# First mixer without GpSimd sums; second block's attention units between its projection steps

## The chip, the cores and the metric

One NeuronCore of one Trainium2 chip. The metric is the device time of one execution in microseconds, the median over runs. TensorE (PE) multiplies, VectorE (DVE), ScalarE (ACT) and GpSimd (POOL) do the rest, and their instructions are ordered among each other by semaphores alone.

## The reference

Two models, one after the other, on 256 tokens of width 1024, all in float32.

- The first has two layers with modulation: `cond @ ada_w` gives shift, scale and gate for each half layer. Layer 0 mixes by 16 attention heads of width 64 with a relative position bias and a block-causal band, layer 1 by spatial gating. Both have a squared-ReLU MLP of width 4096.
- The second has two layers. Each norms x, projects it to aq, ak, av, ag (512 each), bq (512), bk, bv (128 each) and bg (512), and does

```python
lam = exp(sum(lp[0] * lp[1])) - exp(sum(lp[2] * lp[3])) + lam_init
p = softmax(aq_h @ ak_h.T * 64 ** -0.5 + bias)   # 4 heads, two components each
oa = (p[0] - lam * p[1]) @ av_h                  # one value product of the difference
ya = rms_norm(oa, gain) * (1 - lam_init) * silu(ag)
yb = (softmax(q @ k.T * 64 ** -0.5) @ bv) * silu(bg)   # 8 query heads, 2 key heads, RoPE
x = x + rms_norm(concat(ya, yb) @ w_out, gain)
```

## The kernel before

**Precision.** A product of float32 matrices is done by `matmul3` (L1493 to L1495) as three float32r matmuls: high by high, high by low, low by high. Weights come in chunks of 128x2048 in two halves: a transfer into `raw` (4 half slots, SP queue), ScalarE's copy to `w_hi` (L552, `hi_part`), VectorE's difference to `w_lo` (L916, `lo_part`), 4 chunk slots. A projection of 512 columns takes two chunks and 4 steps of 12 matmuls (half, token tile).

**Modulation.** `adastream` holds 48 chunks of 1 MB, loaded by GpSimd's queue into the two slots of `ada_raw`. VectorE sums the 8 tiles of a chunk, each times its column of `cond`, in two accumulators (`ada_sum`, L939 to L947), and counts the chunk in `s_ada`, for which the next loads of GpSimd's queue wait.

**First mixer.** A loop over h = 0 to 18 is written out for all engines. TensorE does a projection or output step, the value product of head h-3, the scores of head h and the transposes of head h-2. VectorE adds the bias and takes the minimum of the negated scores (L1172), ScalarE exponentiates (L671) and copies transposed probabilities (L666), VectorE normalises (L1133). `head_square`, GpSimd's reciprocals (`head_rinv`), `q_heads` (L1036), a transpose, `unit_hi` (L634) and `unit_lo` (L1108) make the operands of scores. Of the modulation chunks 10 to 18, VectorE sums the even ones: 10 whole, ahead of `unit_lo(4)` and `unit_lo(5)`, and 12, 14, 16, 18 in quarters, one to a head. GpSimd sums the odd ones 11, 13, 15, 17 (`pool_sum`, L453 to L459).

**Second block**, for each of two layers. Projections of bk and bv, bq, aq, ak, av, ag, bg come first (the last two are `lproject(12)` and `lproject(14)`), then 16 units (8 differential: head and component; 8 grouped), then both output projections (`lproject(16)` and `lproject(18)`). Iteration i of the unit loop on TensorE:

```python
# i < 8: the bias through the flipped identity, then the fp32 product, in one bank
nc.tensor.matmul(dst, flip[:], t5_h[:, hh, at:at + S], start=True, stop=False)
last = nc.tensor.matmul(dst, aqT[lanes, hh, seg * P:(seg + 1) * P], akT[lanes, hh, :], ...)
# unit i-1: four transposes (L1957); unit i-2: four value products (L1978)
```

VectorE takes the maximum (L1414), copies transposed probabilities out of PSUM (L1424), and scales the outputs by the reciprocal sums, combining the two components of a head in `y_a` (L1434, L1442) and gating `y_b` (L1453). ScalarE exponentiates (L871) and squares `y_a` (L883). GpSimd makes the reciprocals and gates `y_a` (L526, L530) once, after all four heads. `keep_warm` (L1578) adds a small matmul to the late units. After it come the transposes of `y_a` and `y_b`, their high and low halves, and the output projections.

## Time and profile before

| what | value |
|---|---|
| time, median of 3 runs | 1172.77 us (1171.68 to 1174.82) |
| profiled execution, its own time | 1173.97 us |
| its span | 1172.3 us |
| mean granted clock of TensorE | 0.958 |
| TensorE, VectorE, ScalarE, GpSimd busy | 1124.2, 770.9, 527.9, 132.1 us |
| first mixer's head loop | about 87.6 to 189.7 us in the span |
| from ag's projection to the last output matmul | 890.8 to 994.4 and 1060.9 to 1164.6 us |

The span runs from the first to the last instruction; the time of an execution also has what lies around it. Matmuls are pipelined: the duration of one is longer than the distance to the next, so costs on TensorE are read from start to start. The granted clock is given as a share of 2.4 GHz.

### The profile page before, as it was taken

To read this page: it belongs to the slowest core of one execution; us is meant where nothing else is said; L and a number is where in the kernel's file an instruction comes from. 1 tells how busy PE (TensorE), PEld (TensorE's weight loads), DVE (VectorE), ACT (ScalarE), POOL (GpSimd) and SP (SyncE) were. 2 spreads that over 40 slices of the span, in tenths; PEclk is the share of its full clock that TensorE was granted. 3 is DMA by queue.
4 is the path that set the end of the run, shared out by engine and by line. 5 is a ranking of instruction groups with operands and counts; after the bars stand their busy time and mean duration, and the time that the engine had idled before them with its cause. 6 is when DMAs were issued, how large, how long until landed. Compare 5 with 4: busy or idle time off the path is not lost.

```text
span 1172.3 us, 18435 instructions
## 1 busy us (share of the span) xinstructions
PE 1124.2 (96%) x6206; PEld 951.3 (81%) x6206; DVE 770.9 (66%) x1306; ACT 527.9 (45%) x865; POOL 132.1 (11%) x154
## 2 busy tenths in 40 slices
PE   6989799999999999999999999999999999899997
PEld 6867678799989878889997898999788677788675
DVE  5696857787886667687867555545674462763662
ACT  1454433444543457444433454444555442554441
POOL 0124840100000100100000000000110020110020
PEclk9999979799999889999998999999899999799999
DMA  9875553578778358766774446644465100566001
GB/s 370 289 252 197 198 197 111 177 280 301 261 277 296 138 191 291 250 225 215 249 253 152 143 145 209 211 151 135 165 217 180 64 5 19 186 211 201 20 0 45
DMA packets 58071, 219.12 MB, mean 187 GB/s; under 512 B 6532, under 2 KB 12420, under 8 KB 51880
## 3 DMA queue, kind: packets, MB, share of 16 engines
q1 hardware_dynamic: 49232, 170.02, 42.6%
q0 software_dynamic: 5760, 41.95, 10.1%
q10 hardware_dynamic: 3032, 6.57, 1.6%
q8 instruction: 24, 0.39, 0.1%
q14 instruction: 23, 0.19, 0.1%
HBM read 217.46 MB, written 1.06 MB: 186 GB/s over the span
## 4 chain that ended last, share of the span: by engine, by line
PE 75%; issue 8%; DVE 4%; DMA 2%; POOL 2%; ACT 1%; DVEq 0%; ACTq 0%; POOLq 0%
PE ps L1493 21%; PE ps L1494 21%; PE ps L1495 21%; PE ps L1940 1%; PE ps L1938 1%; PE ps L1978 1%; DMA ada_raw<-in_adastream 1%; DVE w_lo L916 1%; PE ps L1578 1%; POOL rinv L429 1%; PE ps L1560 1%; PE ps L1957 1%; PE ps L1542 1%; PE ps L1855 1%; PE ps L1738 1%
## 5 line engine op out<-in xcount | busy, mean ns | idle before, releaser
L916 DVE TENSOR_TENSOR w_lo<-raw,w_hi 128x1024 fp32r<-128x1024 f32 (+1 forms) x318 | 365.6, 1193 | 113.7 <-ACT w_hi L552 106.9
L552 ACT ACTIVATE w_hi<-raw 128x1024 fp32r<-128x1024 f32 (+1 forms) x318 | 307.9, 1009 | 163.4 <-DMA raw<-in_wstream 97.3
L1493 PE MATMUL ps<-h_hi,w_hi 128*128 128x256 f32 x704 | 202.0, 287 | 0.2
L1494 PE MATMUL ps<-h_lo,w_hi 128*128 128x256 f32 x704 | 200.5, 285 | 0.0
L1495 PE MATMUL ps<-h_hi,w_lo 128*128 128x256 f32 x704 | 200.4, 285 | 0.0
L1493 PE MATMUL ps<-w_hi,h_hi 128*128 128x512 f32 (+1 forms) x480 | 192.5, 401 | 3.1 <-DVE h_lo L997 3.1
L1494 PE MATMUL ps<-w_lo,h_hi 128*128 128x512 f32 (+1 forms) x480 | 189.3, 394 | 0.0
L1495 PE MATMUL ps<-w_hi,h_lo 128*128 128x512 f32 (+1 forms) x480 | 188.7, 393 | 0.0
L1493 PE MATMUL ps<-w_hi,a_hi 128*128 128x512 f32 x352 | 137.4, 390 | 1.5 <-DVE a_lo L1318 1.5
L1493 PEld LDWEIGHTS ps<-h_hi,w_hi 128*128 128x128 f32 x704 | 136.3, 194 | 3.1 <-issue 1.7
L1494 PE MATMUL ps<-w_lo,a_hi 128*128 128x512 f32 x352 | 137.2, 390 | 0.0
L1494 PEld LDWEIGHTS ps<-h_lo,w_hi 128*128 128x128 f32 x704 | 136.4, 194 | 0.7
L1495 PE MATMUL ps<-w_hi,a_lo 128*128 128x512 f32 x352 | 137.0, 389 | 0.0
L1495 PEld LDWEIGHTS ps<-h_hi,w_lo 128*128 128x128 f32 x704 | 136.3, 194 | 0.0
L1493 PEld LDWEIGHTS ps<-w_hi,h_hi 128*128 128x128 f32 x480 | 94.8, 198 | 23.1 <-DVE h_lo L997 2.8
L1495 PEld LDWEIGHTS ps<-w_hi,h_lo 128*128 128x128 f32 x480 | 94.5, 197 | 18.9
L1494 PEld LDWEIGHTS ps<-w_lo,h_hi 128*128 128x128 f32 x480 | 94.8, 198 | 17.6
L716 ACT ACTIVATE arena<-ps 128x512 f32<-128x512 f32 x32 | 19.1, 598 | 147.8 <-PE ps L1495 147.8
L1237 DVE TENSOR_TENSOR arena<-arena 128x512 f32<-128x512 f32 x32 | 22.0, 688 | 90.8 <-ACT arena L716 90.8
L1493 PEld LDWEIGHTS ps<-w_hi,a_hi 128*128 128x128 f32 x352 | 66.2, 188 | 15.1 <-issue 2.0
L1495 PEld LDWEIGHTS ps<-w_hi,a_lo 128*128 128x128 f32 x352 | 66.1, 188 | 14.0
L1494 PEld LDWEIGHTS ps<-w_lo,a_hi 128*128 128x128 f32 x352 | 66.2, 188 | 12.9
(177 smaller groups left out, 1387.8 us busy)
## 6 DMA issues: line engine op xcount, KB each, us to landing
raw<-in_wstream SPq DMA_DIRECT2D x296, 512.0 KB, 5.4
ada_raw<-in_adastream POOLq DMA_DIRECT2D x40, 1024.0 KB, 5.5
ada_raw<-in_adastream SPq DMA_DIRECT2D x4, 1024.0 KB, 9.3
arena<-in_adastream SPq DMA_DIRECT2D x4, 1024.0 KB, 10.8
raw<-in_wsmall SPq DMA_DIRECT2D x22, 128.0 KB, 2.1
row<-in_gate_rows ACTq DMA_DIRECT2D x5, 512.0 KB, 4.5
row<-in_params ACTq DMA_DIRECT2D x2, 769.0 KB, 4.1
x<-in_x SPq DMA_DIRECT2D x1, 1024.0 KB, 9.5
```

Of the source, the lines that this page charges most:

```text
L429: nc.gpsimd.tensor_tensor(dst, mean, half[:, 0:cols_n], ALU.pow).then_inc(done, 1)
L552: act.activation(w_hi[:, c % SPLIT, at], raw[:, n, 0:width // 2], ACT.Copy)\
L716: act.activation(relu[:, u, :], ps[:, 4 + u, :], ACT.Relu).then_inc(s_upread, 1)
L916: nc.vector.tensor_tensor(w_lo[:, c % SPLIT, at], raw[:, (2 * c + h) % RAW, 0:width // 2], w_hi[:, c % SPLIT, at].bitcast(F32), ALU.subtract)\
L1237: own.inc(nc.vector.tensor_tensor(squared[:, u, :], relu[:, u, :], relu[:, u, :], ALU.mult))
L1493: nc.tensor.matmul(dst, sh, mh, start=start, stop=False)
L1494: nc.tensor.matmul(dst, sh, ml, start=False, stop=False)
L1495: return nc.tensor.matmul(dst, sl, mh, start=False, stop=stop)
L1542: last = nc.tensor.transpose(ps[:, 4 + pr, b * S + t * P:b * S + (t + 1) * P], xn[:, t, k * P:(k + 1) * P], ident[:])
L1560: last = nc.tensor.matmul(ps[:, bank, b:b + 1], ada_acc[:, a, (b % 2) * P:(b % 2 + 1) * P], ones[:, 0:1], start=True, stop=True)
L1578: nc.tensor.matmul(ps[:, bank, :], zero_row[:], zeros4, start=True, stop=True)
L1738: last = nc.tensor.matmul(ps[:, HEAD_BANK[h], at:at + DH], wideT[:, j % 2, (qt + kb) * P:(qt + kb + 1) * P], v_tok[:, kb, j * DH:(j + 1) * ...
```

## The change

**First mixer.** `pool_sum` is gone and GpSimd only loads. The odd chunks 11, 13, 15, 17 are scaled by ScalarE, half a chunk in each of heads 2, 3, 6, 7, 10, 11, 14, 15, and their 8 scaled tiles are added by VectorE in three instructions at heads 4, 8, 12, 16 (`scaled_sum`). The even chunks 10 to 18 are summed by halves at heads 0, 1, 4, 5 and so on; chunk 10 is moved into the loop.

**Second block.** The operands of the scores are kept as high and low halves, and the scores use `matmul3`. The queries of the differential heads are stored in backward order, and VectorE adds the bias straight from `t5_h` as it takes the minimum. The two components of a head are normalised and subtracted before they are transposed, so four transposed differences and four value products stand in place of eight. ScalarE copies transposed probabilities. The unit loop has 19 iterations and holds the 8 steps of ag and bg (i = 0 to 5, 8, 9) and the first 4 output steps (14 to 17). The evictions of ag and bg with Silu stand inside ScalarE's loop (i = 4, 9). `y_a` is gated head by head on VectorE. `keep_warm` is out of the loop. Output products end in another order of k, so the last four chunks of a layer come in the order 12, 14, 13, 15. Low halves of the operands (`second_lo`) are 7 more instructions on VectorE.

```diff
-POOL_ADA = (11, 13, 15, 17)
+
+SCALED_ADA = {2: 11, 6: 13, 10: 15, 14: 17}
...
                 for k in range(16):
-                    load(C_SECOND + 4 + k, wstream[bass.ds(layer * 16 + (C_SECOND + k), 1)]
+                    row_k = k if k < 12 else (12, 14, 13, 15)[k - 12]
+                    load(C_SECOND + 4 + k, wstream[bass.ds(layer * 16 + (C_SECOND + row_k), 1)]
                          .rearrange("a p n -> p (a n)"), CW, layer * (2 * C_LAYER))
...
-            def pool_sum(a):
-
-                n = POOL_ADA.index(a)
-                pool.wait_ge(s_araw[1], 16 * (a // 2 - 3))
-                v = ada_raw[:, 1]
-                own.inc(nc.gpsimd.tensor_tensor(v, v, cond[:].unsqueeze(2)
-                                                .to_broadcast([P, KT, AW]), ALU.mult))
-                for m in (4, 2):
-                    own.wait()
-                    own.inc(nc.gpsimd.tensor_tensor(v[:, 0:m], v[:, 0:m], v[:, m:2 * m], ALU.add))
-                own.wait()
-                nc.gpsimd.tensor_tensor(ada_acc[:, (a + ADA_AT) % ADA_KEPT, :], v[:, 0], v[:, 1],
-                                        ALU.add).then_inc(s_pool_ada, 1)
...
-            ada_load(adastream[10], 0, 9)
+            ada(10, 1)
             head_rinv(1)
-            ada_load(adastream[11], 1, 10)
-            ada_load(adastream[12], 0, 11)
-            pool_sum(11)
-            ada_load(adastream[14], 0, 12)
+            ada(11, 3)
             head_rinv(2)
-            pool_sum(13)
             head_rinv(3)
-            ada_load(adastream[16], 0, 13)
-            pool_sum(15)
-            pool_sum(17)
-            ada_load(adastream[18], 0, 14)
-            ada(20, 2)
+            ada(14, 8)
...
+                for hh in range(4):
+                    pool.wait_ge(s_yss, layer * 4 + (hh + 1))
+                    v = slice(2 * hh, 2 * hh + 2)
+                    rinv(rinv8[:, 0, v], mean8[:, 0, v], ss8[:, 0, v], P, s_yq)
...
+                if h in (2, 3, 6, 7, 10, 11, 14, 15):
+                    a, q = SCALED_ADA[h - h % 2], h % 2
+                    if q == 0:
+                        act.wait_ge(s_araw[1], 16 * (a // 2 - 3))
+                    for k in range(4 * q, 4 * q + 4):
+                        last = act.activation(ada_raw[:, 1, k], ada_raw[:, 1, k], ACT.Copy,
+                                              scale=cond[:, k:k + 1])
+                    if q == 1:
+                        last.then_inc(s_scaled, 1)
...
+                def evict(j, dst, func, banks):
                     for t in range(TT):
                         ready(j, t)
...
+                evict(3, ak, ACT.Copy, (2, 3))
+                for u, (a, k) in ((1, (2, 0)), (2, (2, 2)), (3, (0, 0)), (4, (0, 2))):
+                    transposed(u, tiles_of(qk2_hi[:, a, k:k + 2]), DH ** -0.5, a == 0)
+                lsplit(12, CW)
+                lsplit(13, CW)
+                evict(4, av, ACT.Copy, (0, 1))
+                for u, k in ((5, 0), (6, 2)):
+                    transposed(u, tiles_of(qk2_hi[:, 1, k:k + 2]), 1.0)
+                lsplit(14, CW)
+                lsplit(15, CW)
...
+                for i in range(18):
+                    if i in (3, 5, 7, 9) or i >= 10:
+
+                        n = (i - 3) // 2 if i < 10 else i - 6
+                        act.wait_ge(s_pT, layer * 12 + (16 + n + 1))
+                        act.wait_ge(s_pv, layer * 12 + (16 + n))
+                        src = ps[:, 6, :]
+                        src = backward(src) if n < 4 else src.rearrange("p (a i) -> p a i", i=P)
+                        act.activation(prob_T.rearrange("p (a i) -> p a i", i=P), src, ACT.Copy)\
+                            .then_inc(s_pTc, 1)
+                    if i < 16:
+                        act.wait_ge(s_max, layer * 16 + (16 + i + 1))
+                        if i == 9:
+                            act.wait_ge(s_comb, layer * 4 + 4)
+                        elif i >= 8:
+                            n = i - 6 if i >= 11 else (i - 3) // 2 + 1
+                            act.wait_ge(s_pT, layer * 12 + (16 + n))
+                        for seg in range(2):
+                            v = slice(seg * S, (seg + 1) * S)
+                            src = prob[:, i % 3, v] if i < 8 else ps[:, 4 + i % 2, v]
+                            last = act.activation(prob[:, i % 3, v], src, ACT.Exp,
+                                                  bias=negmax[:, i % 3, seg:seg + 1],
+                                                  scale=-1.0 if i < 8 else 1.0,
+                                                  accum_out=sums[:, i, seg:seg + 1])
+                        last.then_inc(s_exp, 1)
...
+                    if i == 4:
+                        evict(5, sub_gate, ACT.Silu, (2, 3))
+                    if i == 9:
+                        evict(6, b_gate, ACT.Silu, (0, 1))
...
+            def scaled_sum(a):
+
+                dve.wait_ge(s_scaled, (a - 9) // 2)
+                v = ada_raw[:, 1]
+                for m in (4, 2):
+                    own.inc(nc.vector.tensor_tensor(v[:, 0:m], v[:, 0:m], v[:, m:2 * m], ALU.add))
+                    own.wait()
+                nc.vector.tensor_tensor(ada_acc[:, (a + ADA_AT) % ADA_KEPT, :], v[:, 0], v[:, 1],
+                                        ALU.add).then_inc(s_ada, 1)
 
...
+                if h in (4, 8, 12, 16):
+                    scaled_sum(9 + h // 2)
+                if h in (0, 1, 4, 5, 8, 9, 12, 13, 16, 17):
+                    a, q = 10 + h // 4 * 2, h % 2
+                    marks = ada_part(a, a, range(4 * q, 4 * q + 4), marks if q else ())
...
+                def second_lo(u, lo, hi, scale, back=False):
+
+                    dve.wait_ge(s_qkT, layer * 7 + (8 + u + 1))
+                    bank = ps[:, 4 + u % 4, :]
+                    src = backward(bank) if back else bank.rearrange("p (a i) -> p a i", i=P)
+                    nc.vector.scalar_tensor_tensor(lo, src[:, 0:lo.shape[1]], scale, hi.bitcast(F32),
+                                                   ALU.mult, ALU.subtract).then_inc(s_qk2lo, 1)
+
                 lsplit(9)
...
                 for i in range(16 + 3):
-                    if i < 16:
+                    if i < 8:
                         dve.wait_ge(s_s, layer * 16 + (16 + i + 1))
-                        nc.vector.tensor_reduce(negmax[:, i % 2, :],
-                                                ps[:, i % 2, :].rearrange("p (a b) -> p a b", b=S),
+                        if i in (4, 6):
+                            dve.wait_ge(s_pT, layer * 12 + (16 + (i - 4) // 2 + 1))
+                        if i in (3, 5, 7):
+                            dve.wait_ge(s_comb, layer * 4 + (i - 1) // 2)
+                        own.wait()
+                        dve.sem_inc(s_scores_seen, 1)
+                        for seg in range(2):
+                            v = slice(seg * S, (seg + 1) * S)
+                            at = P - seg * P
+                            last = nc.vector.tensor_tensor_reduce(
+                                prob[:, i % 3, v], ps[:, 4 + i % 2, v], t5_h[:, i // 2, at:at + S],
+                                -1.0, 3e38, ALU.add, ALU.min, negmax[:, i % 3, seg:seg + 1])
...
+                    if i in (2, 4, 6, 8):
+
+                        hh = i // 2 - 1
+                        one, two = 2 * hh, 2 * hh + 1
+                        dve.wait_ge(s_exp, layer * 16 + (16 + two + 1))
+                        own.inc(nc.vector.reciprocal(recip[:, one:two + 1], sums[:, one:two + 1]))
+                        own.wait()
+                        own.inc(nc.vector.tensor_scalar(recip[:, two], recip[:, two], lam[:, 0:1],
+                                                        None, ALU.mult))
+                        for seg in range(2):
+                            v = slice(seg * S, (seg + 1) * S)
+                            own.inc(nc.vector.tensor_scalar(prob[:, one % 3, v], prob[:, one % 3, v],
+                                                            recip[:, one, seg:seg + 1], None,
+                                                            ALU.mult))
+                        own.wait()
+                        for seg in range(2):
+                            v = slice(seg * S, (seg + 1) * S)
+                            last = nc.vector.scalar_tensor_tensor(
+                                prob[:, two % 3, v], prob[:, two % 3, v], recip[:, two, seg:seg + 1],
+                                prob[:, one % 3, v], ALU.mult, ALU.add)
...
+                    if i in (6, 8, 10, 12):
+
+                        hh = (i - 6) // 2
+                        dve.wait_ge(s_yq, layer * 4 + (hh + 1))
+                        dve.wait_ge(s_sub, layer * 2 + 2)
+                        for t in range(TT):
+                            v = y_a[:, t, hh * P:(hh + 1) * P]
+                            last = nc.vector.scalar_tensor_tensor(
+                                v, v, rinv8[:, 0, 2 * hh + t:2 * hh + t + 1],
+                                sub_gate[:, t, hh * P:(hh + 1) * P], ALU.mult, ALU.mult)
...
+                for i in range(19):
+                    if i < 4:
+                        gate_step(12, (2, 3), i // 2, i % 2)
+                    if i in (4, 5):
+                        if i == 4:
+                            pe.wait_ge(s_cp, layer * 12 + 8)
+                        gate_step(14, (0, 1), 0, i - 4)
+                    if i in (8, 9):
+                        gate_step(14, (0, 1), 1, i - 8)
+                    if i == 10:
+                        pe.wait_ge(s_cp, layer * 12 + 10)
+                        pe.wait_ge(s_ya, layer * 4 + 2)
+                        transpose_pair(2, tiles(y_a, 0, 1)).then_inc(s_oT, 1)
+                    if i == 13:
+                        pe.wait_ge(s_ya, layer * 4 + 4)
+                        transpose_pair(3, tiles(y_a, 2, 3)).then_inc(s_oT, 1)
+                    if i == 14:
+                        pe.wait_ge(s_h, layer * 8 + (24 + 2))
+                    if i == 16:
+                        pe.wait_ge(s_cp, layer * 12 + 12)
+                    if 14 <= i <= 17:
+                        out_step(16 + (i - 14) // 2, (i - 14) // 2, i % 2, range(4))
+
...
+                    if i in (4, 6, 8, 10) or i >= 11:
+
+                        n = (i - 4) // 2 if i < 11 else i - 7
+                        pe.wait_ge(s_pTc, layer * 12 + (16 + n + 1))
+                        pe.wait_ge(s_o, layer * 12 + (4 + n))
+                        for seg in range(2):
+                            for kb in range(TT):
+                                at = (seg * 2 + kb) * P
+                                if n < 4:
+                                    dst = ps[:, 7, seg * P:(seg + 1) * P]
+                                    mv = av[:, kb, n * P:(n + 1) * P]
+                                else:
+                                    dst = ps[:, 7, seg * DH:(seg + 1) * DH]
+                                    mv = bv[:, kb, (n % 2) * DH:(n % 2 + 1) * DH]
+                                last = nc.tensor.matmul(dst, prob_T[:, at:at + P], mv,
+                                                        start=kb == 0, stop=kb == 1)
+                        last.then_inc(s_pv, 1)
                     if i < 16:
-
-                        pe.wait_ge(s_exp, layer * 16 + (16 + i - 1))
+                        if i == 0:
+                            pe.wait_ge(s_qk2lo, layer * 7 + 7)
+                        elif 2 <= i < 10:
...
+                                st = (qk2_hi[lanes, 0, hh, q], qk2_lo[lanes, 0, hh, q])
+                                mv = (qk2_hi[lanes, 1, hh, :], qk2_lo[lanes, 1, hh, :])
...
+                    if i in (3, 5, 7, 9) or 10 <= i <= 17:
+
+                        n = (i - 3) // 2 if i < 10 else i - 6
+                        if n < 4:
+                            pe.wait_ge(s_comb, layer * 4 + (n + 1))
+                            slot = (2 * n + 1) % 3
+                        else:
+                            pe.wait_ge(s_exp, layer * 16 + (16 + n + 5))
+                            slot = (n + 4) % 3
+                        pe.wait_ge(s_pTc, layer * 12 + (16 + n))
```

## Rows read from the trace of the kernel before

**Rows 1.** The page: busy time (us, share, instructions), and transfers (KB each, us to landing)

```profile
PE 1124.2 (96%) x6206; PEld 951.3 (81%) x6206; DVE 770.9 (66%) x1306; ACT 527.9 (45%) x865; POOL 132.1 (11%) x154
...
ada_raw<-in_adastream POOLq DMA_DIRECT2D x40, 1024.0 KB, 5.5
```

**Rows 2.** TensorE's waits, 60 to 215 us: total, times, longest

```profile
PE ps L1493 <- DVE k_lo L1108: 4.6, 1, 4.6
PE ps L1552 <- DVE arena L1036: 3.7, 1, 3.7
PE ps L1738 <- DVE k_lo L1108: 2.7, 1, 2.7
...
PE ps L1738 <- ACT both L666: 1.1, 2, 0.7
```

**Rows 3.** Windows, first mixer: length, PE, PEld, DVE, ACT, POOL busy, PEclk, DMA, GB/s

```profile
87.60:189.70 102.10, 91.11 (x461) 75.10 (x462) 70.34 (x165) 45.00 (x109) 50.15 (x33) 0.87 0.53 181
...
140.00:150.00 10.00, 5.73 (x26) 4.47 (x24) 8.85 (x10) 2.19 (x3) 8.79 (x5) 0.71 0.60 206
150.00:160.00 10.00, 9.33 (x40) 7.85 (x39) 4.71 (x20) 4.87 (x13) 3.64 (x1) 0.60 0.61 182
```

**Rows 4.** Timeline of VectorE, first mixer: start, duration, instruction

```profile
116.27 1.22 DVE L916 TENSOR_TENSOR w_lo<-raw,w_hi 128x1024 fp32r<-128x1024 f32 x1
...
119.63 4.01 DVE L916 TENSOR_TENSOR w_lo<-raw,w_hi 128x1024 fp32r<-128x1024 f32 x1
```

**Rows 5.** Timeline of GpSimd, first mixer

```profile
118.96 3.60 POOL L453 TENSOR_TENSOR ada_raw<-ada_raw,cond 128x2048 f32<-128x2048 f32 x1
```

**Rows 6.** Windows, second block: the same stretch of both layers

```profile
890.77:994.39 103.62, 100.51 (x506) 75.80 (x505) 51.02 (x108) 41.85 (x115) 9.63 (x9) 0.98 0.17 54
1060.92:1164.55 103.63, 100.52 (x506) 75.66 (x504) 50.92 (x108) 41.79 (x115) 9.63 (x9) 0.98 0.16 50
```

**Rows 7.** Timeline of TensorE, units of the second block's layer 0

```profile
912.64 0.59 PE L1938 MATMUL ps<-ada_raw,flip 128*128 128x256 f32 x2
...
922.66 0.60 PE L1938 MATMUL ps<-ada_raw,flip 128*128 128x256 f32 x2
...
925.07 0.66 PE L1957 MATMUL ps<-ident,both 128*128 128x128 f32 x4
...
926.46 0.60 PE L1938 MATMUL ps<-ada_raw,flip 128*128 128x256 f32 x2
...
954.58 0.38 PE L1578 MATMUL ps<-zero_row 1*128 1x512 bf16 x1
...
957.38 0.38 PE L1578 MATMUL ps<-zero_row 1*128 1x512 bf16 x1
```

**Rows 8.** Groups by form: count, busy us, mean ns of one, idle before

```profile
L943 DVE SCALAR_TENSOR_TENSOR ada_acc<-ada_raw,cond,ada_acc 128x256 f32 x84 | 40.1, 477 | 0.0
...
L1414 DVE TENSOR_REDUCE negmax<-ps 128x2 f32<-128x512 f32 x32 | 22.1, 691 | 43.1 <-PE ps L1940 30.4 <-PE ps L1945 12.8
...
L823 ACT ACTIVATE arena<-ps 128x512 f32<-128x512 f32 x12 | 6.3, 608 | 0.0
...
L1172 DVE CUSTOM_DVE_ANT_0 both<-ps,gate 128x256 f32<-128x256 f32 x8 | 3.4, 419 | 0.0
...
L823 ACT ACTIVATE ada_raw<-ps 128x256 f32<-128x256 f32 x2 | 0.8, 378 | 0.0
```

**Rows 9.** Timeline of TensorE, first mixer: scores of one head

```profile
179.84 0.32 PE L1493 MATMUL ps<-qk_hi 64*128 64x128 f32 x1
...
180.72 0.55 PE L1757 MATMUL ps<-ident,both 128*128 128x128 f32 x3
```

**Rows 10.** Timeline of ScalarE: table load, then exponentials of two units

```profile
915.93 1.28 ACT L871 ACT_TABLE_LOAD   x1 [2.50 <-DVE negmax L1414]
917.23 0.47 ACT L871 ACTIVATE both<-ps,negmax 128x256 f32<-128x256 f32 x1
...
919.29 1.05 ACT L552 ACTIVATE w_hi<-raw 128x1024 fp32r<-128x1024 f32 x1
```

321 lines of the change are left out of this document (149 added, 172 removed).

## The prediction

> **What bounds the kernel now.** I read the page first. TensorE is busy for 96% of the span [rows 1], so only two things can shorten the run: less TensorE work, or the removal of TensorE's waits and of the slow spells around them. I then took TensorE's waits by window, which puts nearly all of them in the first mixer and at the ends of blocks. In the mixer there are six kinds of wait, 15.5 us in all; the reader should see that the longest end on VectorE, in the low halves of the keys (`k_lo`) and in normalised heads (`arena`) [rows 2]. The windows say what follows the waits: over the mixer's 102.1 us the granted clock is 0.87 on average, and ten microseconds with TensorE busy for 9.33 run at 0.60, right after ten with 5.73 [rows 3]. Missing clock is 102.1 x 0.13 = 13.3 us. Then I asked what VectorE was doing before those waits: one `w_lo` subtraction takes 1.22 us, the same one takes 4.01 us [rows 4] while GpSimd multiplies a whole modulation chunk for 3.60 us [rows 5]. I count some 15 us of such stretching under the four GpSimd sums.
>
> In the second block the picture is the other one. From the start of the ag projection to the last output matmul a layer takes 103.6 us, with TensorE busy for 100.5 of them at clock 0.98, and both layers agree to 0.01 us [rows 6]. So TensorE is the limit there. The two gate projections (ag, bg) are 8 steps of 12 matmuls and end at 912.64, which is 21.87/8 = 2.73 us a step. A differential unit then costs 3.80 us (922.66 to 926.46), of which transposes and value products are 1.39, so its fp32 scores with the position bias are 2.41. A late grouped unit costs 2.80 [rows 7].
>
> **The mixer, part by part.** (a) The GpSimd sums go; four times 4 to 5 us of stretched VectorE work goes with them. (b) ScalarE now scales the four odd chunks: 8 copies of 128x256 at 0.38 us each (about 0.29 start to start, as they overlap) [rows 8], 1.3 us in each of eight heads. ScalarE is busy for 45 of the 102 us [rows 3], so this is mostly hidden; in heads 6 and 7 it stands before `head_square`, `out_hi` and `unit_hi`, and I charge 1 us for each of these two. (c) VectorE adds the scaled chunks: 128x1024, 128x512 and 128x256, by the 1.22 us for 1024 elements [rows 4] about 2.4 us with waits, four times 2.4 = 9.6. Its total falls by 15 and rises by 9.6. (d) Chunk 10 moves from before the low key halves into heads 0 and 1: two multiplies and six multiply-adds of about 0.4 us and a final add, 3.4 us, leave the front of the 4.6 us wait. (e) GpSimd's queue: the load of chunk 13 now stands before the reciprocals of the q square sums, and it waits for VectorE's sum of chunk 11 at head 4. That makes the 3.7 us wait of head 6 about 1 us longer. Later loads are issued some two heads before use, against 5.5 us to land [rows 1]; these I leave at no cost, hidden under two heads of 3.3 us, else 2 us each.
>
> Waits: 15.5 - 3.4 (d) - 3.6 (most of the waits for the low halves at head 8, as VectorE comes 4 us earlier) - 2.5 (late normalised heads) + 1 (e) + 3. The last is new: heads 8 and 9 now hold a scaled sum, two half chunks and a weight half, about 9.5 us of VectorE work for two heads against 4 to 7 us on TensorE, and head 12 waits for a head normalised at head 11. That makes 10.0, so 5.5 less. Clock: in proportion, 13.3 x 10.0/15.5 = 8.6, so 4.7 less. With the 2 us of (b): **-8 us**. Bounds: -15 (half of the remaining waits go too), -2 (VectorE's new work fills all that the sums left).
>
> **The second block, part by part, for each layer.** Scores become three float32r products over 64 rows, six matmuls of 256 columns. No row shows that shape. The nearest is a mixer head, three of 128 and three of 256 columns in 0.88 us [rows 9]; the six big ones lie between 0.72 (0.12 each) and 1.17 (0.88 x 256/192), and I take 0.9, near the 0.12 to 0.16 us from start to start that the row's matmuls have. The eight differential units become four differences ahead of the transposes, so 12 sets of transposes and value products in place of 16. `keep_warm` goes. TensorE's work is then 16 steps x 2.73 = 43.7, scores 16 x 0.9 = 14.4, 12 x 1.39 = 16.7, transposes of `y_a` and `y_b` 2.0: **76.8 us against 103.6**, so 26.8 less if everything else hides.
>
> It doesn't. I wrote the three queues side by side, with row prices: add-and-minimum with the bias 0.42 for 256 elements, maximum 0.69, ScalarE copy of a bank 0.61 (0.5 start to start), multiply-add of 256 elements 0.48 [rows 8], two exponentials of a unit about 1.0 [rows 10]. A difference is two multiplies, two multiply-adds and two tiny ones, 2.0 us. The results:
> - i = 0 to 5: six steps of 2.73 cover everything; no wait.
> - i = 6, 7: no step. VectorE has 0.8 (minimum), 0.4 (copy of the output), 2.0 (difference); transposes wait for the difference, the value product for ScalarE's copy. TensorE idles about 3.6 us.
> - i = 8, 9: steps again, no wait.
> - i = 9 to 13: no step until 14. ScalarE has four bank copies (2.2), four units of exponentials (4.1), two pairs of squares (2.0, like exponentials), two gate evictions (1.2), two weight halves (2.1), one operand half (0.6) and two table loads of 1.28 (2.6) [rows 10]: 14.8 us against 2.3 us a unit on TensorE. Also the single output bank 7 chains value product, scores, maximum, output and next value product, 0.9 + 0.9 + 0.25 + 0.6 + 0.35 + 0.45 = 3.45 us a unit. And step 14 waits for a square, GpSimd's reciprocal, the gating, a transpose and a split of `y_a`. TensorE idles about 9.2 us.
> - i = 14 to 17 hold the output steps, 5.05 us each on TensorE, which cover the chain; the last two units and `y_b` cost 0.9.
>
> Idle is 13.7, so the stretch is 90.5 at full clock: 13.1 less. The idle shares (half of i = 9 to 13, half of i = 6, 7) are like that of the ten microseconds before the 0.60 stretch [rows 3], so I expect the clock at 1.2 GHz for part of i = 8 and of i = 11 to 14. About 13 us of such work takes twice as long, half of that hidden behind ScalarE: 6.5 back. **-6.6 us a layer, -13.2 for both.** Bounds: -13.1 a layer (no slow spell), -1 (all of it slow).
>
> Seven VectorE subtractions for the low halves (0.7 each, like a maximum) stand before units whose weights have been split long before; hidden under the 10.9 us projections, else 5 us. GpSimd's two products with the gain (1.3 us each) now run beside VectorE's differences and may stretch them by 2 to 3 us as in [rows 4, 5]; inside the bounds. The order of the last four weight chunks costs nothing: each load is issued over 5 us ahead. The final residual keeps its chain.
>
> Table loads: the exponential is left for the gate's function twice in the loop, so 5 loads a layer instead of 2. The row shows 1.28 us, and the next activation starts 0.02 after it [rows 10]. The Trainium skill (ScalarE: Activation LUTs, What ACT_TABLE_LOAD costs) adds a drain of some 1.38 us to every switch, 2.66 in all; by it the sum would be worse by three times 1.38 a layer, 8.3 us. The trace shows no such gap there, so the sum goes by the row.
>
> **Sum.** The profiled execution took 1173.97 us, 1.67 more than its span, and 1.2 more than the median of 1172.77. 1173.97 - 8 - 13.2 = 1152.8, and less the 1.2: **1152 us**.
>
> **Rivals.**
> - A, the units stay bound: the chain of ScalarE and VectorE with a slow clock through i = 6 to 15 returns the whole saving, only the mixer gains. For it: the half idle window. Against: the output steps are a busy 20 us. 1172.8 - 8 = 1165 us. Chance 0.13.
> - B, no slow spell, and the mixer reaches its bound: 1172.8 - 26 - 13 = 1134 us. For it: the layers now run at 0.98 with 3 us of idle time in all [rows 6]. Against: I expect 14. Chance 0.17.
> - C, a drain on every table switch: 1.28 more on six loads in all, by the length of the load itself, 7.7 us: 1160 us. Against: the 0.02 us gap. Chance 0.05. The Trainium skill's rule is named above.
> - D, slower: the one output bank. Its chain is 3.45 us a unit at full clock; if it keeps TensorE so idle that the clock stays low through i = 8 to 17, the 10.9 us of output steps in there double and some 7 us of the chain is not hidden: 103.6 - 13.1 + 18 = 108.5 a layer. Both layers then give 10 back, more than the mixer's 8: 1175 us. It decides once low clock costs 17 us a layer. Against: the output steps are 20 us without a pause. Chance 0.05; no change 0.05.
> - My forecast, 1140 to 1162: 0.55.
>
> Range: 1132 to 1168. A measurement of this kernel can tell about 0.3% (3.5 us) from no change. Faster 0.89, same 0.05, slower 0.06.
>
> **What would show it.** After: a `w_lo` subtraction is never above 1.3 us in the mixer; VectorE's wait before the keys' scores is near 1 us; mixer some 8 to 10 us shorter. In a layer: 76 to 78 us of TensorE work at full clock; the stretch about 97; idle around i = 6, 7 and i = 10 to 13 behind ScalarE and VectorE; granted clock under 0.9 there. I am wrong if scores cost over 1.2 us, if a step waits for a weight chunk, or if ScalarE's table loads come in other places.

## The result and the profile after

The changed kernel takes 1160.57 us (median of 4 runs, 1155.58 to 1162.09) against 1173.8 us beside it: a ratio of 0.987, 95% interval 0.984 to 0.990. The forecast was 1152 us in a range of 1132 to 1168, so the sign and the range hold; the point is 8.6 us too low. Measured a second time the ratio was 0.988 (0.986 to 0.991).

The profiled execution took 1160.94 us. The page of it, to set beside [rows 1]: TensorE lost 28.8 us of busy time (1124.2 to 1095.4) but the span only 13.0, so it is busy for 94% and no longer for 96%.

```profile
span 1159.3 us, 18344 instructions
...
PE 1095.4 (94%) x6096; PEld 942.7 (81%) x6096; DVE 767.2 (66%) x1364; ACT 557.3 (48%) x925; POOL 92.1 (8%) x146
```

The windows of the three changed stretches: from the mixer's first scores to the last transposes of its output, and from the first gate step to the last output matmul of both layers. A layer's stretch ends here where a next matmul would start; counted so, it was 103.5 us before, 0.1 less than in [rows 6]. They answer to [rows 3] and [rows 6]. Columns: stretch, length, busy time of PE, PEld, DVE, ACT, POOL, then granted clock, DMA share, GB/s.

```profile
81.22:180.38 99.16, 88.95 (x460) 73.53 (x461) 68.43 (x186) 57.41 (x141) 12.34 (x17) 0.90 0.55 184
884.24:983.67 99.43, 88.04 (x451) 71.89 (x449) 46.23 (x123) 50.22 (x129) 8.08 (x13) 0.88 0.17 55
1051.17:1150.76 99.59, 88.00 (x451) 71.90 (x449) 46.25 (x123) 50.22 (x129) 8.09 (x13) 0.88 0.17 53
```

The reader should do one sum on the second row. TensorE is busy for 88.0 us and idle for 11.4. Of the clock, 12% is missing, 11.9 us. Part of that falls on idle time, where it costs nothing: taken in windows of 1 us, each window's missing clock times its busy share, 9.5 us fall on busy time, and the work at full clock is 88.0 - 9.5 = 78.6 us. The same sum on the layer before gives 98.7 of work, 3.1 of idle and 1.7 of missing clock. So a layer lost 20.1 us of work, but gained 8.3 of idle time and 7.8 of slow clock: of 20 us, 4 arrive.

TensorE's waits in the mixer, to set beside [rows 2]: `k_lo` before the first scores fell from 4.6 to 1.2 us, the wait of head 6 for its normalised heads (`arena`) rose from 3.7 to 4.5, and there is a wait of 2.5 for the last normalised heads. The wait at head 12 that I had added isn't there. Of `k_lo`, the line of L1569 is the wait at the first scores, that of L1814 the one at head 8.

```profile
PE ps L1628 <- DVE arena L1050: 4.5, 1, 4.5
PE ps L1628 <- DVE row L1147: 2.5, 1, 2.5
PE ps L1814 <- DVE k_lo L1122: 1.2, 1, 1.2
PE ps L1569 <- DVE k_lo L1122: 1.2, 1, 1.2
```

The low halves of the weights on VectorE from 86 to 181 us: minimum, median and maximum of 15 in nanoseconds. None is stretched, where [rows 4] had one of 4.01 us and the second row below, also of the kernel before, is another.

```profile
L930 DVE TENSOR_TENSOR w_lo<-raw,w_hi x15: 1212/1216/1226, 86.6 to 180.2; 128x1024 fp32r<-128x1024 f32 x15
```

```profile
137.82 4.53 DVE L916 TENSOR_TENSOR w_lo<-raw,w_hi 128x1024 fp32r<-128x1024 f32 x1
```

TensorE's waits in the second layer's stretch (total, times, longest). The value products (L2061) wait for ScalarE's copy of the transposed probabilities, a set of transposes for VectorE's difference, the first output step for the low half of `y_a`.

```profile
PE ps L2061 <- ACT both L860: 4.9, 5, 1.7
PE ps L2097 <- DVE both L1509: 2.9, 1, 2.9
PE ps L1569 <- DVE h_lo L1019: 2.9, 1, 2.9
PE ps L1628 <- DVE arena L1520: 0.9, 1, 0.9
```

And the first layer in windows of 4 us: the units i = 6 to 8 (913 to 921), then i = 11 to the first output steps (929 to 957).

```profile
913.00:917.00 4.00, 1.69 (x8) 1.49 (x9) 3.93 (x16) 3.73 (x9) 0.98 (x2) 0.91 0.31 102
917.00:921.00 4.00, 4.00 (x17) 3.23 (x16) 0.61 (x1) 2.13 (x9) 0.89 (x2) 0.67 0.42 132
...
929.00:933.00 4.00, 2.33 (x18) 1.89 (x17) 2.68 (x5) 3.96 (x6) 0.78 (x2) 1.00 0.50 163
933.00:937.00 4.00, 2.89 (x15) 2.27 (x14) 1.93 (x5) 4.00 (x14) 0.00 (x0) 0.54 0.10 33
937.00:941.00 4.00, 3.55 (x15) 2.81 (x14) 1.33 (x5) 1.68 (x5) 0.89 (x2) 0.50 0.00 0
...
949.00:953.00 4.00, 3.30 (x8) 2.63 (x9) 0.57 (x1) 0.00 (x0) 0.00 (x0) 0.50 0.13 35
953.00:957.00 4.00, 4.00 (x26) 3.44 (x24) 0.62 (x2) 0.04 (x1) 0.00 (x0) 0.90 0.01 4
```

Each idle stretch is followed by a spell at 1.2 GHz: a short one behind i = 7, and one of 20 us from i = 11 on, which ends only some 4 us into the dense output steps that begin at 949.7. Six score matmuls of a unit, one row of the timeline each (start, length; two are left out), cost 0.89 us from 887.15 to the next step at 888.04:

```profile
887.15 0.38 PE L1569 MATMUL ps<-qk_hi 64*128 64x256 f32 x1
887.37 0.28 PE L1570 MATMUL ps<-qk_lo,qk_hi 64*128 64x256 f32 x1
...
887.84 0.27 PE L1571 MATMUL ps<-qk_hi,qk_lo 64*128 64x256 f32 x1
888.04 0.50 PE L1569 MATMUL ps<-w_hi,h_hi 128*128 128x512 f32 x1
```

### The profile page after: what moved, and what is told of

It is laid out like the page before. It is cut to its first block, busy times and chain, and to the rows that moved or that the text cites. A ratio compares the mean times of both kernels' runs of the same rounds, so it can differ in the third digit from the quotient of the medians.

```text
span 1159.3 us, 18344 instructions
## 1 busy us (share of the span) xinstructions
PE 1095.4 (94%) x6096; PEld 942.7 (81%) x6096; DVE 767.2 (66%) x1364; ACT 557.3 (48%) x925; POOL 92.1 (8%) x146
## 4 chain that ended last, share of the span: by engine, by line
PE 75%; issue 10%; DVE 7%; ACT 4%; POOL 2%; DMA 2%; DVEq 0%; ACTq 0%; SPq 0%; POOLq 0%
PE ps L1569 22%; PE ps L1570 22%; PE ps L1571 22%; DVE w_lo L930 2%; PE ps L1664 2%; PE ps L1654 1%; PE ps L1636 1%; PE ps L1618 1%; POOL rinv L437 1%; PE ps L1931 1%; ACT w_hi L530 1%; ACT ada_raw L660 1%; PE ps L1628 1%; DMA arena<-in_adastream 1%; ACT both L872 1%
## 5 line engine op out<-in xcount | busy, mean ns | idle before, releaser
L930 DVE TENSOR_TENSOR w_lo<-raw,w_hi 128x1024 fp32r<-128x1024 f32 (+1 forms) x318 | 358.5, 1169 | 58.9 <-ACT w_hi L530 52.9
L1569 PE MATMUL ps<-w_hi,h_hi 128*128 128x512 f32 (+1 forms) x480 | 195.7, 408 | 8.9 <-DVE h_lo L1019 5.8
L1569 PE MATMUL ps<-h_hi,w_hi 128*128 128x256 f32 x704 | 203.2, 289 | 0.6 <-DVE h_lo L1011 0.4
L1569 PEld LDWEIGHTS ps<-h_hi,w_hi 128*128 128x128 f32 x704 | 137.6, 195 | 3.7 <-issue 2.2
L1569 PE MATMUL ps<-w_hi,a_hi 128*128 128x512 f32 x352 | 137.4, 390 | 0.7 <-DVE a_lo L1337 0.7
L1569 PEld LDWEIGHTS ps<-w_hi,h_hi 128*128 128x128 f32 x480 | 94.9, 198 | 30.5 <-issue 8.9
L1569 PEld LDWEIGHTS ps<-w_hi,a_hi 128*128 128x128 f32 x352 | 66.2, 188 | 14.2 <-issue 1.2
```

Of the source, the lines that this page charges most:

```text
L930: nc.vector.tensor_tensor(w_lo[:, c % SPLIT, at], raw[:, (2 * c + h) % RAW, 0:width // 2], w_hi[:, c % SPLIT, at].bitcast(F32), ALU.subtract)\
L1569: nc.tensor.matmul(dst, sh, mh, start=start, stop=False)
```

## The experiments

### Which part gives what, and what is chance

The parts alone. `e1_mixer` is the kernel before with the mixer's part: in short

```diff
-            ada_load(adastream[11], 1, 10)
-            ada_load(adastream[12], 0, 11)
-            pool_sum(11)
+            ada(11, 3)
...
+                if h in (4, 8, 12, 16):
+                    scaled_sum(9 + h // 2)
```

> The kernel before with the mixer's part of the change alone. The prediction's sum gives -8 us for this part. In the trace of the changed kernel the out projection's end comes 9.3 us earlier (190.80 for 200.07), but the start of the second block only 5.0 us earlier (832.00 for 836.98). Theory 1, the mixer's gain is kept and the 4.3 us belong to chance at the later stage boundaries: 1164 to 1166 us. Theory 2, the boundaries give half of it back every time, because the clock falls there at another phase: about 1169 us. The second block's two stretches must stay at 103.6 us each.

`e2_block` is the changed kernel with the mixer's lines turned back, so that GpSimd sums again.

> The changed kernel with the mixer of before: the second block's part alone. The prediction gave -13.2 us for it (-6.6 a layer). The trace of the changed kernel shows stretches of 99.7 us a layer, 3.9 less than before, so theory 1 says about -8 us, 1165 us; if the stretches came out at 97 as predicted when the mixer doesn't shift the clock's phase, 1160 us (theory 2). TensorE busy 88 us of a stretch at clock 0.88 expected by theory 1.

`e11_after_again` has no edit.

> The changed kernel itself once more, on the same chip as the two kernels beside it. It shows how far the stage boundaries ahead of the second block vary between executions while its two stretches stay. By the first profile: stretches 99.4 and 99.6 us, ratio to the kernel before 0.984 to 0.990; a ratio of 0.992 or more would say that part of the first measurement's gain was chance.

Ratios to the kernel before: 0.995 (0.992 to 0.998) for the mixer alone, -6.0 us of 1177; 0.995 (0.992 to 0.999) for the second block alone, -5.4 us; 0.988 for both. The runs of one kernel spread over 7 to 15 us here, so the landmarks of the five profiles say more. They are read off TensorE's timeline, in us; the two rows with two numbers are the two layers.

```
stage                                before        after         mixer alone    block alone    after again
first projection starts              42.93         39.63         40.04          43.02          42.69
from there to the first MLP matmul   173.4         167.4         164.6          177.1          163.7
from there to the second block       620.7         625.0         625.1          625.0          625.3
second block until its gate steps    53.8, 54.2    52.2, 54.3    52.3, 54.2     52.2, 54.3     54.3, 52.3
gate steps to last output matmul     103.5, 103.5  99.4, 99.6    103.5, 103.5   99.4, 99.6     99.6, 99.2
between the layers                   12.4          13.2          12.7           13.1           13.0
behind the last output matmul        7.9           8.5           7.8            8.6            8.5
```

The first row has two values 3 us apart, and the changed kernel shows both: its first profile had the early one, so 3.3 of the 9.3 us that it showed at the end of the mixer need not be the edit's. The second row holds the mixer: 173.4 and 177.1 us with GpSimd's sums; without them 163.5 to 167.4 in the nine profiles that have just this mixer, with a mean of 164.6. By the means that is -10.6 us. But the two old values differ by 3.7 us among themselves; 2.9 of that is the wait of head 6 for its normalised heads, 3.7 us in one profile and 6.6 in the other. And the third row counts too: 620.7 and 625.0 with the old mixer, 625.0 to 626.3 in the nine with the new one, mean 625.8. Over both rows together the old mixer takes 794.1 and 802.1 us, the new one 789.2 to 792.4, mean 790.4: -7.7 us by the means, but -3.7 or -11.7 by the one or the other old profile. So two profiles of the old mixer can't decide between the two theories of the first experiment; the whole runs say -6.0 with an interval from 2.7 to 9.3, which holds both. The fifth row repeats to 0.4 us: each layer gains 4.0 us, and the two rows below it cost some 0.7 each. The block's part is worth -2 x 4.0 + 0.7 + 0.7 = -6.6 us, half of the -13.2 foreseen. By the stretches theory 1 of the second experiment holds; the whole run gained 5.4 where that theory said 8. The landmarks' sum, -7.7 - 6.6 = -14.3 us, agrees with the two measurements of both parts (-14.9 and -13.7).

### Is it the idle time, or the clock behind it?

`e3_warm` puts idle matmuls on zeros into the waits:

```diff
+                        if i == 6:
+                            pe.wait_ge(s_cp, layer * 12 + 10)
+                            keep_warm(3, 3)
+                        if i in (11, 12):
+                            pe.wait_ge(s_cp, layer * 12 + 12)
+                            keep_warm(1, 6 if i == 11 else 5)
                         pe.wait_ge(s_pTc, layer * 12 + (16 + n + 1))
...
+                        if i == 7:
+                            keep_warm(3, 10)
```

> The changed kernel with idle matmuls on zeros (as keep_warm) where TensorE waits in the second block's loop: 3 and 10 at i=6 and 7, 6 and 5 at i=11 and 12, 4 at i=13, 11 before the first out step. Nothing else changes. A stretch holds 11.6 us of idle time and 12.0 us of missing clock (99.7 x 0.12). Theory 1, the missing clock follows from the idle stretches: the granted clock of the stretch rises to 0.95 or more, the stretch falls to about 90 to 93 us, the run to 1142 to 1150 us. Theory 2, ScalarE's and VectorE's chain sets the stretch and the slow clock is hidden behind it: clock up, stretch still 98 to 100 us, run 1158 to 1163 us. Theory 3, the fillers come late and push the units back: slower than 1163.

`e6_dense` has the same fillers in the same number, but each is `matmul(ps[:, bank, :], w_hi[:, c, 0:128], w_hi[:, c, 0:512])` on a weight chunk that lies ready.

> The same places and counts as the run with idle matmuls on zeros (3, 10, 6, 5, 4 and 11), but each filler is a matmul of 128 rows by 128 by 512 float32r columns on a weight chunk. The run with zeros left the granted clock at half from i=11 for 26 us although TensorE was busy for all of it. Theory 1, the clock looks at what the matmuls do, not at whether the engine is busy: with dense fillers the spells at i=8 and at i=11 to 14 go, the stretch's clock is above 0.96, and the stretch is 92 to 95 us against 105.8 with zeros. Theory 2, the clock falls because of what the units are made of (transposes, products of 64 columns) and no filler in the gaps helps: stretch 104 to 107 us as with zeros.

What the fillers compute is never read. Ratios: 0.996 (0.994 to 0.999) with zeros, 0.978 (0.973 to 0.982) with dense fillers; 1173.4 and 1149.2 us. In windows of 4 us with zeros:

```profile
929.00:933.00 4.00, 3.23 (x24) 2.51 (x22) 3.56 (x6) 3.77 (x11) 0.89 (x2) 1.00 0.29 87
933.00:937.00 4.00, 3.26 (x16) 2.23 (x17) 1.69 (x4) 3.97 (x9) 0.00 (x0) 0.83 0.36 112
937.00:941.00 4.00, 4.00 (x15) 2.23 (x14) 1.83 (x5) 2.61 (x9) 0.00 (x0) 0.50 0.00 0
...
949.00:953.00 4.00, 4.00 (x18) 3.38 (x17) 0.76 (x2) 0.00 (x0) 0.00 (x0) 0.50 0.13 33
953.00:957.00 4.00, 4.00 (x11) 1.42 (x11) 2.30 (x4) 2.00 (x6) 0.00 (x0) 0.50 0.12 35
957.00:961.00 4.00, 4.00 (x10) 2.50 (x9) 0.00 (x0) 0.00 (x0) 0.00 (x0) 0.50 0.00 0
```

and with dense ones:

```profile
932.00:936.00 4.00, 4.00 (x19) 3.45 (x18) 0.20 (x1) 3.44 (x7) 0.00 (x0) 0.65 0.12 33
936.00:940.00 4.00, 4.00 (x28) 3.30 (x27) 1.96 (x6) 3.03 (x10) 0.72 (x2) 1.00 0.00 0
940.00:944.00 4.00, 3.54 (x26) 2.95 (x24) 2.77 (x7) 1.51 (x5) 0.17 (x1) 1.00 0.02 4
944.00:948.00 4.00, 3.73 (x19) 2.73 (x19) 3.06 (x6) 2.00 (x6) 0.00 (x0) 1.00 0.16 37
```

With zeros TensorE is busy for all of 937 to 961 and stays at half clock; eleven fillers, 2.5 us at full clock, then cost 4.87 us in one piece. The stretch grows from 99.4 to 105.7 (theory 3). With dense fillers the second spell lasts 3.4 us instead of 20 and the stretch is 93.9 at clock 0.98 (theory 1), though the same 39 fillers take some 9 us of it. So at least 5.5 us of what the slow clock costs isn't hidden behind the other engines, of the 9.5 us that fall on busy time. The Trainium skill (TensorE: Matmul & The Clock Gate, Part 1) describes the gate as one that goes by how busy the array has been recently. These rows show a TensorE that the profile calls busy at half clock for 24 us, so the profile's busy time alone doesn't tell the two runs apart, and here the measurement decides. The two kinds of filler differ in three things at once: one row against 128, zeros against data, bf16 against float32r. Which of them matters was not tried.

### What idles TensorE there?

Four edits, one each. `e4_no_silu`:

```diff
-                        evict(5, sub_gate, ACT.Silu, (2, 3))
+                        evict(5, sub_gate, ACT.Copy, (2, 3))
```

and the same for `b_gate`. This kernel leaves out the gates' Silu, so its output is another one; it serves for the time alone.

> The changed kernel with Copy in place of Silu in the two gate evictions inside the second block's loop, so that the gates are left linear (that part of the computation is left out) and the four table loads inside the loop (4 x 1.28 = 5.1 us of ScalarE a layer) are gone. Theory 1, ScalarE's chain sets the waits at i=6, 7, 11 and 12 (6.7 us of the 11.6 us idle a layer stand right behind the loads): idle time falls by 4 to 6 us a layer and the slow spell at i=8, 9 with it, run 1146 to 1152 us. Theory 2, the loads lie beside waits that VectorE sets anyway: within 2 us of the changed kernel, 1158 to 1162 us.

The table loads that it takes out, on ScalarE's timeline of the changed kernel (start, length):

```profile
1073.93 1.28 ACT L835 ACT_TABLE_LOAD   x1
1075.23 1.09 ACT L835 ACTIVATE arena<-ps 128x512 f32<-128x512 f32 x2
1076.20 0.60 ACT L860 ACTIVATE both<-ps 128x512 f32<-128x512 f32 x1
1076.82 1.28 ACT L872 ACT_TABLE_LOAD   x1
1078.12 0.51 ACT L872 ACTIVATE both<-both,negmax 128x256 f32<-128x256 f32 x1
```

Four loads of 1.28 us a layer go, and the stretch falls by 1.0 us, to 98.4. The whole run took 1159.0 us, ratio 0.985 (0.981 to 0.989). The wait for the difference stays at 2.9. Theory 2: the loads lie beside waits that VectorE sets. Each activation starts 0.02 us after its load, as the prediction's row had it. The Trainium skill (ScalarE: Activation LUTs, What ACT_TABLE_LOAD costs) has a further drain there; no gap of that kind stands in these rows.

`e5_order` moves the block of the value product behind the block of the scores within a turn:

```diff
-                    if i in (4, 6, 8, 10) or i >= 11:
-                        n = (i - 4) // 2 if i < 11 else i - 7
...
                     if i < 16:
...
                         last.then_inc(s_s, 1)
+                    if i in (4, 6, 8, 10) or i >= 11:
+                        n = (i - 4) // 2 if i < 11 else i - 7
```

> The changed kernel with TensorE's scores of unit i placed ahead of the value product of that turn, so that the product has the 0.9 us of scores between the transposes it needs and itself. Ten waits of a layer's value products for ScalarE's copy of the transposes add up to 4.7 us a layer. Theory 1, the latency of that copy is what idles TensorE: some 3 us a layer less idle, the run 6 us or more below the changed kernel. Theory 2, ScalarE's queue is full and the copy comes no earlier: the same time as the changed kernel within 2 us, the wait moves to the transposes or the scores.

`e8_spread` puts steps where VectorE is late:

```diff
-                    if i in (4, 5):
+                    if i in (5, 7):
...
-                        gate_step(14, (0, 1), 0, i - 4)
+                        gate_step(14, (0, 1), 0, (i - 5) // 2)
```

> The changed kernel with two gate steps moved from i=4 and 5 to i=5 and 7, ahead of the two places where transposes wait for VectorE's difference (2.9 us at i=7). Theory 1, VectorE is only late because it stood idle during i=4 and 5: the waits at i=6 and 7 (3.7 us a layer) go and with them the slow spell at i=8 (1.7 us), 4 to 5 us a layer. Theory 2, VectorE's work of i=4 to 7 is as long as TensorE's with the steps in it: a wait of 2 us or more at i=7 stays, and the gain is under 2 us a layer.

`e7_half` cuts the output steps:

```diff
+                early = {12: ((0, 0, 0),), 13: ((0, 1, 0),), 14: ((1, 1, 0), None, (0, 0, 2)),
+                         15: ((1, 0, 0), (0, 1, 2)), 16: ((1, 0, 2),), 17: ((1, 1, 2),)}
...
-                        out_step(16 + (i - 14) // 2, (i - 14) // 2, i % 2, range(4))
+                            out_step(16 + cb, cb, t, range(k0, k0 + 2))
```

> The changed kernel with the first four output steps cut in halves of six matmuls, two of them moved to i=12 and 13 and one ahead of the wait at i=14, where TensorE stood idle and the clock was at half; the second pair of y_a is transposed into bank 0. The same work in all. Theory 1, the slow spell of 20 us begins and lasts because no dense work stands at i=10 to 13: it gets shorter by half and the stretch falls from 99.7 by 5 to 8 us, the run by 10 to 16 us. Theory 2, the chain of ScalarE, VectorE and the one output bank sets i=10 to 18: the moved work is missing later and the stretch stays within 2 us.

Stretches of the first layer, in the order order, half, spread, no Silu:

```profile
887.67:983.21 95.54, 87.33 (x451) 70.70 (x449) 46.57 (x123) 50.19 (x129) 7.16 (x13) 0.89 0.18 58
```
```profile
881.45:977.35 95.90, 85.36 (x451) 69.55 (x448) 46.17 (x123) 50.20 (x129) 8.08 (x13) 0.93 0.18 56
```
```profile
887.08:983.51 96.43, 87.53 (x451) 71.34 (x448) 46.23 (x123) 50.33 (x129) 8.08 (x13) 0.89 0.18 57
```
```profile
887.63:986.06 98.43, 88.22 (x451) 72.19 (x449) 46.25 (x123) 45.10 (x125) 7.33 (x13) 0.88 0.18 57
```

Against 99.4: -3.9, -3.5, -3.0 and -1.0 us. The whole runs, on one chip beside the kernel before: 0.980 (0.977 to 0.984) for the order, 0.984 (0.980 to 0.987) for the halves, 0.983 (0.979 to 0.987) for the spread steps. By busy time and clock, the first works mostly through idle time (8.2 for 11.4 us, missing clock 10.5 for 11.9): the way from the transposes through ScalarE's copy to the product had nothing beside it on TensorE. That is theory 1 of its expectation. The second works through the clock (missing 6.7 for 11.9 us); 10.5 us are still idle, and the wait for `y_a`'s low halves is 2.6 us, now in two pieces. Its 3.5 us are less than the 5 to 8 of its theory 1 and more than the 2 of theory 2. The third takes the wait of 2.9 us for the difference away and with it the slow spell at i = 8 (the steps at i = 8 and 9 take 2.8 us each); a wait of 0.8 for the copy stays at i = 7. So VectorE was late because of where the steps stood, and not because its work was too long; 3.0 us are less than the 4 to 5 of theory 1, whose waits and spell did go. The halves' run gained less than its stretches say: 4 to 5 us against the changed kernel by the ratios, where 2 x 3.5 would be 7.

### One queue in the mixer

```diff
-            ada(11, 3)
+            ada(11, 2)
             head_rinv(2)
+            ada(13, 1)
             head_rinv(3)
```

> The changed kernel with GpSimd's reciprocals of the third q chunk ahead of the load of modulation chunk 13, which waits for VectorE's sum of chunk 11 at head 4. In the changed kernel that load is issued at 105.98 us and the reciprocals follow until 110.93, the transposes of head 6 wait 4.5 us. Theory 1, as in step (e) of the prediction, the queue is the cause: the reciprocals end about 4 us earlier, the wait falls by 2 us or more (then VectorE's own order sets it), the mixer by 2 to 4 us. Theory 2, VectorE's queue (sums, two part sums, a weight half) would hold the normalised heads anyway: wait 4 us or more. The whole time may not show 2 us against the spread of the runs; the wait in the trace decides.

In the changed kernel the load stands before the reciprocals, on GpSimd's timeline:

```profile
105.98 0.53 POOL L416 DMA_DIRECT2D ada_raw<-in_adastream  x1 [15.31 <-DVE ada_acc L1180]
106.58 0.47 POOL L434 TENSOR_SCALAR mean<-ss 128x8 f32<-128x8 f32 x1
...
109.29 1.64 POOL L437 TENSOR_TENSOR rinv<-mean,half 128x8 f32<-128x8 f32 x1
```

The load's own wait for VectorE's sum of chunk 11 (15.31 us, up to 105.98) thus holds the reciprocals back. With the edit the reciprocals end 3.4 us after VectorE's second sum of squares (109.5 against 106.1) and not 7.6 (110.9 against 103.3), so the queue was the cause as step (e) had it. But the wait of head 6 falls only from 4.5 to 3.2 us, and the mixer not at all that can be seen (164.9 us on the stage of the table's second row, for 164.6 on average): VectorE's own queue, with the sum of the scaled chunk and four products of the next ahead of the normalisation, holds the heads until 111.9. The ratio is 0.986 (0.983 to 0.988). The cause is the one of theory 1, but the wait falls by 1.3 us and not by 2 or more, because VectorE's queue, as in theory 2, comes next.

### A better order

`e10_all` has the edits of `e5_order`, `e7_half`, `e8_spread` and `e9_rinv`.

> The changed kernel with four edits together: scores ahead of the value products, output steps cut in halves and two moved to i=12 and 13, two gate steps at i=5 and 7, reciprocals ahead of the load in the mixer. Alone, the first three took 3.4 to 3.9, 3.5 and 3.1 us off a layer's stretch. If they are independent (theory 1) the stretch is 89 to 90 us and the run 20 to 25 us below the changed kernel, 1133 to 1140 us. If they share one cause, the slow spell of i=11 to 14, whose removal is paid once (theory 2), the stretch is 93 to 95 us and the run 1144 to 1150 us. A lower bound is TensorE's work at full clock, 76 us.

`e12_fill` corrects it:

```diff
-                early = {12: ((0, 0, 0),), 13: ((0, 1, 0),),
+                early = {13: ((0, 0, 0), (0, 1, 0)),
...
+                        if i in (11, 12):
+                            pe.wait_ge(s_cp, layer * 12 + 12)
+                            chunk_in(C_SECOND + 16, layer, C_LAYER)
+                            dense(1, 5 if i == 11 else 3, 16)
```

> The kernel with the four edits (stretch 92.0 us, run 1140 us) with one step corrected: the half step at i=12 waited 3.0 us for the low half of y_a and the clock fell behind it, so it goes to i=13, and 5 and 3 dense matmuls on a weight chunk (128 rows, 512 float32r columns, 1.8 us in all at full clock) stand ahead of the value products of i=11 and 12. The four edits alone left 7 us idle and 6.4 us of missing clock a layer. Theory 1, the slow spell of 929 to 946 us follows from the idle time at i=11 and 12: clock above 0.97, stretch 87 to 90 us, the run 4 to 10 us below 1140. Theory 2, the chain of ScalarE and VectorE through y_a now sets i=10 to 14: the wait turns up at the half steps of i=13 and 14, stretch 91 us or more, no difference in the run beyond 2 us.

The two stretches, `e10_all` first:

```profile
882.23:974.24 92.01, 85.18 (x451) 68.46 (x448) 46.21 (x123) 50.05 (x129) 8.35 (x13) 0.93 0.19 60
```
```profile
883.11:969.97 86.86, 81.85 (x459) 66.03 (x457) 46.22 (x123) 49.93 (x129) 8.36 (x13) 1.00 0.20 64
```

The four edits give 1140.2 us, 0.971 (0.967 to 0.975); the corrected order gives **1134.4 us, 0.967 (0.964 to 0.970)**, 26 to 28 us below the changed kernel by the medians, 24 to 25 by the ratios, and the fastest here. In `e10_all` the 92.0 us lie between the two theories: the savings of 3.9, 3.5 and 3.0 add up to 10.4 but 7.4 come, because the wait had moved with the half step to i = 12, still 3.0 us long, and the clock fell behind it:

```profile
PE ps L1570 <- DVE h_lo L1020: 4.4, 2, 3.0
PE ps L2089 <- ACT both L861: 2.1, 2, 1.3
```

With eight dense fillers and the half step a turn later the clock doesn't fall in the whole stretch, in either layer. 5.1 us for 1.8 us of filler: theory 1. The run made both changes at once, so it doesn't say what each of them gives.

## Why the prediction was right, and where its sizes were off

- **Mixer, -8 predicted; -6.0 measured alone, -7.7 in the landmarks.** The size is right as far as two profiles of the old mixer can tell. (a) holds: no `w_lo` above 1.23 us. (d) to the digit: `k_lo` at the first scores 4.57 to 1.21 us, 3.4 less. At head 8 the waits fell from 4.3 to 1.2 us, 3.0 less for my 3.6. (e): head 6 at 4.5, expected about 4.7. Wrong are the late normalised heads: from 1.8 us the waits there went to 3.5 (1.0 and 2.5), where I took 2.5 off; and the new wait of 3 us at head 12 didn't come. These two errors of 4.2 and 3 us, one each way, mostly cancel, which is luck: waits of 11.4 us from the first scores to the last transposes where I had 10.0. The granted clock of the mixer is 0.90 for 0.87, 10 us missing for my 8.6.
- **Second block, TensorE's work.** 76.8 us predicted, from start to start. A unit's scores cost 0.89 us for my 0.9. The busy time at full clock is 78.6 us, and in `e12_fill`, where the clock never falls, 81.9 with 1.8 of fillers in it, so 80.1. Busy time counts a matmul to its modelled end and so has a tail at every pause; whether the 2 to 3 us are such tails or work that I left out is not settled. The 26.8 us that I expected to save counted the old layer's 3.1 us of idle time and 1.7 of slow clock as work.
- **Second block, idle time.** 13.7 predicted. Found are 11.4 us in the first layer and 11.6 in the second, and up to 2 more if the tails are counted here. In the second layer, predicted and found: i = 6, 7: 3.6 and 3.7 (0.8 and 2.9). i = 9 to 13 with the wait at 14: 9.2 and 7.1. The end: 0.9 and 0.8. The places and the engines are those named. At i = 9 to 14 both reasons that it gave are there: of 6.9 us in the first layer, 3.1 end on ScalarE's copy and 3.8 on VectorE's work on `y_a`. But ScalarE's queue of 14.8 us is not what sets the length: `e4_no_silu` takes two table loads, 2.6 us, out of it and as much at i = 4, and the stretch falls by 1.0.
- **Second block, the clock: two sizes wrong, one against the other.** "About 13 us of such work takes twice as long, half of that hidden behind ScalarE: 6.5 back." The place, i = 8 and i = 11 to 14, was right. On busy time 9.5 us of clock are missing and not 13. With the clock held up by fillers the stretch falls by 5.5 us although the fillers need 9 us of it. So of the 9.5 us at least 5.5 lengthen the stretch and at most 4.0 are hidden, where I had 6.5 hidden. The net cost lies between 5.5 and 9.5 us, and my 6.5 is in there partly by luck. By the terms as counted, 78.6 + 11.4 + 9.5 makes the 99.4 (to 0.1), where I had 76.8 + 13.7 + 6.5 = 97. A layer gained 4.0 instead of 6.6, and how much of the miss is clock and how much work isn't settled: no run has the changed order at full clock without fillers.
- **Why the range held.** The two layers missed by 5.2 us together, the gap and the end by 1.4 more, the mixer by 0 to 2. All of them miss the same way and make up the 8.6 us nearly, in a range of 36 us.
- **What I had left out.** The gap between the layers and the end behind the last matmul each grew by 0.7 us, where I had the residual at no change. The order of the last output steps was changed there, but no experiment separates this; `e2_block` has the growth and `e1_mixer` has not, so it belongs to the second block's part.
- **The rivals.** A, the units stay bound at 1165: nearer to the 1160.6 than the forecast was, since the second block gave only half of its part; but it isn't bound, for 3.9 us a layer come from the order of two blocks alone. B would have needed the clock: at full clock and with the order of `e12_fill` a stretch is 86.9 us, below the 90.5 that I had put there. Its sum takes 13 for the mixer, where the bound was 15. C names 1160 us, nearly the time that came, but its mechanism, a drain at every table switch, isn't in the rows: the number alone would mislead. D, the one output bank: no wait for it is in the list of waits, so nothing shows its 3.45 us chain at work.

## What to carry to other kernels

Work taken off the bounding engine is worth only what doesn't come back as idle time and as missing clock. Split each stretch before and after into work, idle time and slow clock, in small windows so that clock missing in idle time isn't counted as a cost: it names the next step. Then look where dense work can stand: a step between a hand-over to another engine and its return, a half step a turn later, and only as the last means a filler, of the dense kind, since the one on a zero row didn't hold the clock here.

## What the chip showed that I had not expected

- In `e3_warm` TensorE was busy without a pause from 937 to 961 us and had half the clock. What the fillers were made of made the difference: 39 on zeros with a stationary tile of one row, 105.7 us at 0.85; 39 dense ones in the same places, 93.9 us at 0.98.
- In the changed kernel the spell of 20 us ended 4 us after dense work had begun, at 949.7, and not before, though transposes and products of units ran through it.
- The first projection starts at 39.6 to 40.0 us in six of fourteen profiles and at 42.7 to 43.0 in the other eight, with the old mixer (late both times) or the new one (early and late). 3 us of a comparison of two profiles can be that. The two kinds part between 19 and 22 us: a pair of 32-row matmuls takes 1.02 to 1.10 us in all six early profiles and 1.86 in all eight late ones. Here the changed kernel in its two profiles, early and late, with the matmul behind the pair:

```profile
18.98 1.02 PE L1674 MATMUL ps<-both 32*4 32x512 f32 x2
19.93 11.35 PE L1664 MATMUL ps<-cond,arena 128*128 128x1 f32 x61
```
```profile
19.36 1.86 PE L1674 MATMUL ps<-both 32*4 32x512 f32 x2
21.15 10.19 PE L1664 MATMUL ps<-cond,arena 128*128 128x1 f32 x47
```

The granted clock can't settle this, for its record has a hole. In the late profiles it says 1.00 from 10 to 46 us, but at 44 us the projection's matmuls start 0.43 us apart, nearly twice the 0.23 of full clock; the early profiles have the same 0.43, with the clock shown at half:

```profile
10.00:46.00 36.00, 36.00 (x146) 30.75 (x147) 23.22 (x53) 10.56 (x17) 3.32 (x6) 1.00 0.93 367
```
```profile
44.13 0.63 PE L1569 MATMUL ps<-w_hi,h_hi 128*128 128x512 f32 x1
44.56 0.63 PE L1570 MATMUL ps<-w_lo,h_hi 128*128 128x512 f32 x1
```

A clock that fell earlier in the late profiles would fit the pair above; it is not shown. The granted clock of a whole span (0.931 and 0.943 for the same changed kernel) carries this hole with it.
